# Moving gate projections into the first and last steps of a software-pipelined RWKV stage, one core of Trainium2

## The chip, the cores and the metric

One core of one Trainium2 chip runs the whole program in one launch. The time is the device time in microseconds (us). TensorE does the matmuls, VectorE (DVE), ScalarE (ACT) and GpSimd (POOL) the rest; weights come from device memory (DRAM) by DMA, issued from the SP queue, and small transfers are issued from ACT's queue.

## The reference, cut to what matters

Two transformer blocks, one after the other, on 512 tokens of width 1024, all in float32. The stage at issue is the first block's mixer:

```python
h = rmsnorm(x, norm_mix_pre)
f_att, f_rwkv, f_gate = split(h @ w_in)               # 2304, 3328 and 2048 columns
o_att  = dilated_window_attention(q, k, v, rel_bias)  # of f_att
o_rwkv = rwkv7_time_mix(token_shift(f_rwkv, mu), ...) # 16 heads of 64: r, k, v and three small low-rank inputs
gates  = sigmoid(f_gate + b_gate)                     # gate 0 and gate 1, 1024 columns each
merged = gates[0] * (o_att @ w_att_branch) + gates[1] * (o_rwkv @ w_rwkv_branch)
x = x + rmsnorm(merged @ w_out, norm_mix_post)
```

`token_shift` mixes each projected row with the row before it, per channel. Inside `rwkv7_time_mix` a 64x64 state per head runs over the tokens; the kernel does it in 4 chunks of 128 tokens, with a triangular inverse per chunk and head. A feed-forward part follows, and then the second block.

## The kernel before, in words

Every float32 projection is done as three float32r matmuls (lines 526 to 528: high times high, high times low, low times high). Weights come in 126 units of 128 x 2048 float32 (1 MB) through a ring of three buffers. For each unit ACT writes the rounded high part (`hi`, line 1123), and then POOL (line 517), or for ten of the units DVE (`weights_low`, line 1772), writes what is left, the low part.

The stage has these parts in order: q, k and v projections; the dilated attention; then steps -2 to 7 of the RWKV part (`step(p)`, one such function in each engine's program). The 16 RWKV heads are 8 pairs. Step p works on three pairs at once: pair c = p + 2 is prepared (low-rank inputs, decay, key norms), for pair b = p + 1 the triangular inverse is built over seven levels (`level_x`, `level_t`, line 862 and lines 870 and 872), and for pair a = p the four chunks are run through the state (`chunk_rhs`, `chunk_solve`, `chunk_out`) and normalised. So steps -2 and -1 lack a, step -2 lacks b as well, step 6 has no c and step 7 only a. The branch projections `attb` and `rwkvb` follow.

The remaining projections of `h` fill the gaps. They are cut into 42 halves of units: a half is 8 pieces, each three matmuls with 512 columns. They are two low-rank inputs, r, k and v of each pair (24), gate 0 (8) and gate 1 (8). Sixteen are done beside the attention. The other 26 are spread over the steps by `advance(early, n)` and `advance(late, n)`: two in steps -2, -1 and 5, four in each of steps 0 to 4, none in steps 6 and 7. In the steps all halves use bank 0, so the first piece of a half waits until the one before is taken out (`half_taken`). A half of r, k or v is taken by ACT (`stage`, line 1247, into the single buffer GT) and then by DVE (`shift`, lines 1729 and 1730); a gate half by ACT alone (a sigmoid into GT, line 1254 or 1263), which then stores it to DRAM. After every second half ACT runs `hi` for the unit two further on.

The order on each engine is written out by hand and engines wait for each other by semaphores. In step -2 ACT takes both last gate 0 halves before the exponentials of pair 0, and waits for a store before it takes the second, since both use GT. Units 21 and 22 (`attb` and the first of `rwkvb`) have their low parts made by POOL in step 5. Before step 6 ACT issues the loads of both gates from DRAM, into the buffers of the high and low parts of `h`, which no half needs any more.

Of the kernel before, what the change touches and what calls it, by code (L numbers as in the profile page):

```python
# [49 lines left out]
STAGES = [("qk", 6, 6), ("v", 3, 3), ("lora", 1, 0), ("rwkv_first", 4, 0), ("gate0", 4, 0), ("rwkv", 12, 0),  # L50
# [4 lines left out]
SIDE = ("lora", "rwkv_first", "gate0", "rwkv")  # L55

PACKED = ("qk", "v", "lora", "rwkv_first", "rwkv", "gate0", "attb", "rwkvb", "wout", "ffn", "pool", "q2", "kv2",
          "group", "gatep", "gatea", "poolb", "attnb", "wout2", "ffn2")
UNIT0, USE0, UNITS, USES = {}, {}, {}, {}
# [8 lines left out]
def packed_order():  # L68

    at, place = 0, {}  # L70
    for name in PACKED:
        count = UNITS[name]
# [14 lines left out]
    return [place[name, u] for name, count, _ in STAGES for u in range(count)]  # L87
# [80 lines left out]
def build(nc, x, wpack, lora_wa, lora_g, params, rel_bias, post_gains, sink, ctab, btab, icount, out):  # L168
# [7 lines left out]
    with ExitStack() as ctx:  # L176
# [202 lines left out]
        source = packed_order()  # L379


        DVE_LO0, DVE_LO1 = UNIT0["rwkv"] + 2, UNIT0["rwkv"] + UNITS["rwkv"]
# [10 lines left out]
        def half(pair, part):  # L393

            return 2 + 4 * pair + part + (2 * UNITS["gate0"] if pair >= 2 else 0)

        GATE0 = 10

        def half_taken(n):

            if n < 2:
                return shifted, n + 1
            if GATE0 <= n < GATE0 + 8:
                return gated, 2 + n - GATE0 + 1
            late = n >= GATE0 + 8
            pair, part = (n - 2 - 8 * late) // 4, (n - 2 - 8 * late) % 4
            return (gated, pair + 1 + 8 * late) if part == 3 else (shifted, 2 + 3 * pair + part + 1)
# [80 lines left out]
        def _(sp):  # L488
            def load(n):
                if n >= RING:  # L490
                    sp.wait_ge(*freed[n - RING])
                sp.dma_start(raw[:, n % RING, :], wpack[source[n]]).then_inc(unit_in[n % RING], 16)
# [28 lines left out]
        def _(pe):  # L521
# [227 lines left out]
            def later_halves(n0, n1):  # L749
                for n in range(n0, n1):  # L750
                    yield from side_half(n, 0, n - 1)
# [204 lines left out]
            def step(p):  # L956
# [3 lines left out]
                if p == -2:  # L960
                    early = later_halves(GATE0 + 6, GATE0 + 8)
                else:
                    early = later_halves(half(c, 2), half(c, 2) + (2 if 2 <= c < PAIRS else 0))
                late = later_halves(half(c + 1, 0), half(c + 1, 0) + (2 if 2 <= c + 1 < PAIRS else 0))
# [4 lines left out]
                if has_a:  # L969
                    chunk_rhs(a, 0)  # L970
                advance(early, 2)
# [4 lines left out]
                advance(early, 2)  # L976
                if has_a:
                    chunk_out(a, 0)
                for t in range(1, NT):
# [4 lines left out]
                    advance(early, 1)  # L984
                    if has_c:
                        if t == 1:
                            lora_z(c, 1)
                        elif t == 2:
                            key_sums(c)
                        else:  # L990
                            key_roots(c)
# [4 lines left out]
                    advance(early, 1)  # L996
                    if has_a:
                        chunk_out(a, t)
                    advance(early, 2)
# [4 lines left out]
                advance(late, 1)  # L1004
# [4 lines left out]
                advance(late, 3)  # L1009
# [3 lines left out]
                advance(late, 1)  # L1013
# [5 lines left out]
                advance(late, 3)  # L1019
# [3 lines left out]
                advance(late, 1)  # L1023
# [5 lines left out]
                advance(late, 2)  # L1029
                if has_c:  # L1030
                    gate_z(a, c)
                advance(late, 1)
# [3 lines left out]
                advance(late, 2)  # L1036
# [4 lines left out]
                advance(late, 2)  # L1041
                assert next(early, None) is None and next(late, None) is None
# [71 lines left out]
        def _(act):  # L1114
# [5 lines left out]
            def hi(n):  # L1120

                act.wait_ge(unit_in[n % RING], 16 * (n // RING + 1))
# [1092 lines left out]
```

## Time and profile before

| | us |
|---|---|
| three runs of the kernel | 2155.59, 2163.86, 2168.63 (median 2163.86) |
| the profiled execution | 2157.88 |
| its span | 2156.1 |
| TensorE busy | 2025.7 (94%) |
| VectorE busy | 890.8 (41%) |
| ScalarE busy | 792.5 (37%) |
| GpSimd busy | 537.1 (25%) |
| mean granted TensorE clock | 0.93 of full |

The page shows busy time per engine, the span in 40 slices with the busy share and the granted clock, the chain of work that ended last, and the costliest groups of instructions. TensorE's matmuls are pipelined, so its busy time holds latencies that overlap; the rate of work is read from the starts of neighbouring matmuls. "PE" is TensorE.

### The profile page before, as it was taken

The page shows a single profiled execution, that of the slowest core. Times are in us where ns is not written, and L with a number is a line of the kernel's source. Part 1 is how long each engine was busy: PE and PEld are TensorE (multiplying, and loading weights), DVE is VectorE, ACT ScalarE, POOL GpSimd, SP SyncE. Part 2 cuts the span into 40 slices and gives each one's busy share as a digit, 9 for nine tenths or more (in the row PEclk, how much of TensorE's full clock was granted, in tenths as well). Part 3 has the DMA queues.
Part 4 walks back from the last instruction along what each step waited for, and adds up shares of the span by engine and source line. Part 5 has one row for each costly group of instructions (what it writes and reads, how often), then busy time and mean ns, then how long its engine had stood idle before and what let it go on. Part 6 is the DMA issues. An engine that isn't in the chain of part 4 may idle for free.

```text
span 2156.1 us, 24479 instructions
## 1 busy us (share of the span) xinstructions
PE 2025.7 (94%) x10404; PEld 1651.9 (77%) x10404; DVE 890.8 (41%) x1439; ACT 792.5 (37%) x1142; POOL 537.1 (25%) x120
## 2 busy tenths in 40 slices
PE   7999977999999989989989999989899999999998
PEld 5877756778777777877878888878566778888886
DVE  2023335666666666543331144450566432012243
ACT  5235544354354344231342222242465333222222
POOL 2431210000000000002434444433222343444442
PEclk9999995999899998568999999999999999999999
DMA  4621120010010010201332222223111222222222
GB/s 154 221 74 56 67 79 11 23 47 25 23 47 25 23 45 25 79 1 69 117 108 98 98 98 96 94 84 107 39 59 59 84 83 99 97 97 98 98 98 78
DMA packets 31281, 160.80 MB, mean 75 GB/s; under 512 B 3103, under 2 KB 5535, under 8 KB 14916
## 3 DMA queue, kind: packets, MB, share of 16 engines
q1 hardware_dynamic: 19244, 135.40, 18.4%
q10 hardware_dynamic: 11928, 23.83, 3.2%
q8 instruction: 83, 1.36, 0.3%
q14 instruction: 26, 0.21, 0.0%
HBM read 152.63 MB, written 10.25 MB: 76 GB/s over the span
## 4 chain that ended last, share of the span: by engine, by line
PE 83%; DVE 10%; ACT 4%; issue 1%; DMA 1%; POOL 0%; DVEq 0%; ACTq 0%
PE ps L526 21%; PE ps L528 20%; PE ps L527 20%; PE ps L872 2%; PE ps L870 2%; PE ps L619 2%; PE ps L862 2%; PE ps L641 2%; DVE stat L1705 1%; DVE level L1845 1%; PE ps L633 1%; PE ps L912 1%; PE ps L902 1%; PE ps L793 1%; PE ps L950 1%
## 5 line engine op out<-in xcount | busy, mean ns | idle before, releaser
L517 POOL TENSOR_TENSOR w_lo<-w_raw,w_hi 128x2048 fp32r<-128x2048 f32 x116 | 536.9, 4629 | 1588.9 <-ACT w_hi L1123 1588.9
L526 PE MATMUL ps<-ht_hi,w_hi 128*128 128x512 f32 (+1 forms) x1304 | 529.3, 406 | 36.5 <-DVE rkv L1730 22.3
L528 PE MATMUL ps<-ht_hi,w_lo 128*128 128x512 f32 (+1 forms) x1304 | 504.4, 387 | 0.0
L527 PE MATMUL ps<-ht_lo,w_hi 128*128 128x512 f32 (+1 forms) x1304 | 504.3, 387 | 0.0
L1123 ACT ACTIVATE w_hi<-w_raw 128x2048 fp32r<-128x2048 f32 x126 | 241.0, 1914 | 493.6 <-PE ps L528 437.6
L526 PEld LDWEIGHTS ps<-ht_hi,w_hi 128*128 128x128 f32 x1304 | 251.9, 193 | 114.4 <-issue 53.3
L528 PEld LDWEIGHTS ps<-ht_hi,w_lo 128*128 128x128 f32 x1304 | 251.8, 193 | 49.6
L527 PEld LDWEIGHTS ps<-ht_lo,w_hi 128*128 128x128 f32 x1304 | 252.9, 194 | 40.2 <-issue 1.4
L2052 DVE TENSOR_TENSOR hid_lo<-hidden,hid_hi 128x1024 fp32r<-128x1024 f32 x27 | 129.3, 4789 | 149.1 <-ACT hid_hi L1485 149.1
L526 PE MATMUL ps<-w_hi,hid_hi 128*128 128x512 f32 x432 | 168.2, 389 | 0.0
L528 PE MATMUL ps<-w_hi,hid_lo 128*128 128x512 f32 x432 | 168.1, 389 | 0.0
L527 PE MATMUL ps<-w_lo,hid_hi 128*128 128x512 f32 x432 | 168.0, 389 | 0.0
L1346 ACT ACTIVATE tinv_t<-ps 128x512 fp32r<-128x512 f32 x96 | 57.7, 601 | 117.5 <-PE ps L872 117.5
L526 PEld LDWEIGHTS ps<-w_hi,hid_hi 128*128 128x128 f32 x432 | 81.1, 188 | 16.9
L527 PEld LDWEIGHTS ps<-w_lo,hid_hi 128*128 128x128 f32 x432 | 81.1, 188 | 16.8
L528 PEld LDWEIGHTS ps<-w_hi,hid_lo 128*128 128x128 f32 x432 | 81.1, 188 | 16.8
L526 PE MATMUL ps<-w_hi,ht_hi 128*128 128x512 f32 (+2 forms) x256 | 86.7, 339 | 2.1 <-POOL w_lo L517 2.1
L528 PE MATMUL ps<-w_hi,ht_lo 128*128 128x512 f32 (+2 forms) x256 | 86.5, 338 | 0.0
L527 PE MATMUL ps<-w_lo,ht_hi 128*128 128x512 f32 (+2 forms) x256 | 86.3, 337 | 0.0
L1867 DVE TENSOR_TENSOR xinv<-ps,consts 128x512 fp32r<-128x512 f32 x96 | 62.5, 684 | 45.0 <-PE ps L862 44.4
L1845 DVE TENSOR_TENSOR level<-gram_inv,consts 128x512 fp32r<-128x512 f32 x112 | 80.5, 760 | 0.6
L2061 DVE TENSOR_TENSOR hidden<-ps,gate_act 128x1024 f32<-128x1024 f32 x16 | 19.6, 1225 | 135.3 <-ACT gate_act L1524 135.3
(253 smaller groups left out, 2814.7 us busy)
## 6 DMA issues: line engine op xcount, KB each, us to landing
w_raw<-in_wpack SPq DMA_DIRECT2D x126, 1024.0 KB, 4.9
bias_skewed_dram<-bias_rows_dram ACTq DMA_DIRECT2D x1, 3840.0 KB, 22.4
toe<-bias_skewed_dram ACTq DMA_DIRECT2D x1, 3072.0 KB, 13.0
gate_dram<-gate_tile ACTq DMA_DIRECT2D x10, 256.0 KB, 5.0
x_res<-in_x SPq DMA_DIRECT2D x4, 512.0 KB, 6.5
merged<-gate_dram ACTq DMA_DIRECT2D x1, 2048.0 KB, 8.7
gate<-gate_dram ACTq DMA_DIRECT2D x1, 2048.0 KB, 14.7
x_res<-in_x ACTq DMA_DIRECT2D x1, 2048.0 KB, 8.8
```

The costliest lines, as they stand in the source:

```text
L517: nc.gpsimd.tensor_tensor(Wl[:, slot, :], raw[:, slot, :], f32(Wh[:, slot, :]), ALU.subtract).then_inc(lo_ready, 1)
L526: mm(dst, wh, ah, start=first, stop=False)
L527: mm(dst, wh, al, start=False, stop=False)
L528: return mm(dst, wl, ah, start=False, stop=last)
L619: last = mm(bank(s["bank"], s["n"]), s["q"], s["k"], start=True, stop=True)
L641: last = mm(out_slot(a, i), v, PT[:, j, :], start=j == 0, stop=j == len(it["vals"]) - 1)
L862: last = mm(ps[:, 4 + h, tok(t)], Mb[h][:, t, :], Tb[h][:, t, :] if lv else identR[:], start=True, stop=True)
L1123: actf(Wh[:, n % RING, :], raw[:, n % RING, :], ACT.Copy).then_inc(hi_ready, 1)
L1346: actf(TT[h][:].rearrange("p a b -> p (a b)"), bank(6 + h), ACT.Copy)
L1845: inc(v.tensor_tensor(Mb[h][:], GA[h][:], lmask(lv), ALU.mult), "m_ready")
L1867: inc(v.tensor_tensor(Xb[h][:], b3(4 + h), cast4(ident), ALU.add), "x1_ready")
L2052: v.tensor_tensor(HIl[:, 2 * g:2 * g + 2, :], HID[:, 2 * g:2 * g + 2, :], f32(HIh[:, g % RING, :, :]), ALU.subtract).then_inc(hid_lo, 1)
```

## The change

The halves get an explicit order (`HALVES`) and each step a list of halves (`STEP_HALVES`). Beside the attention: the low-rank inputs, r, k, v of pairs 0 and 1, and all of gate 0. Step -2: gate 1 halves 0 and 1. Step -1: two halves of pair 2. Steps 0 to 4: three halves each, all r, k or v. Step 5: v of pair 7 and gate 1 half 2. Step 6: three gate 1 halves. Step 7: the last two. How many pieces run at each of 21 places in a step is in three tables. TensorE's `chunk_rhs(a, 0)` now comes ahead of `inverse_grams(b)`, and the first pieces of a step after `level_x(b, 0)` and after `chunk_out(a, 0)`; `key_roots` moves behind `level_t(b, 3)`. The last half of a step is taken at the start of the next. Gate 1 halves 2 to 7 each get a buffer of their own. Twelve units are loaded as two strided halves of 512-byte rows. DVE makes the low parts of 13 units (10 to 22) and none is left to POOL inside the steps. The loads of the two gates move into step 7, behind the last stored gate half.

```diff
+HALVES = ([("lora", 0, 0), ("lora", 0, 1)] + [("rkv", pair, part) for pair in range(2) for part in range(3)]
+          + [("gate0", u, 0) for u in range(8)] + [("gate1", u, 0) for u in range(2)]
+          + [("rkv", pair, part) for pair in range(2, PAIRS) for part in range(3)]
+          + [("gate1", u, 0) for u in range(2, 8)])
...
+STEP_HALVES = {-2: (16, None, 17), -1: (18, None, 19), 5: (35, None, 36), 6: (37, 38, 39), 7: (40, 41, None)}
+STEP_HALVES.update({p: (20 + 3 * p, 21 + 3 * p, 22 + 3 * p) for p in range(5)})
+
+SLOTS3 = (0, 1, 2, 1, 1, 1, 1, 1, 0, 1, 1, 2, 1, 2, 1, 1, 1, 2, 1, 1, 2)
+SLOTS2 = (0, 1, 2, 1, 1, 1, 1, 1, 0, 0, 0, 0, 1, 1, 1, 1, 1, 1, 1, 1, 0)
+SLOTS_LAST = (2, 2, 2, 1, 1, 0, 1, 2, 1, 2, 2, 0, 0, 0, 0, 0, 0, 0, 0, 0, 0)
...
-        DVE_LO0, DVE_LO1 = UNIT0["rwkv"] + 2, UNIT0["rwkv"] + UNITS["rwkv"]
+        DVE_LO0, DVE_LO1 = UNIT0["rwkv"] + 1, UNIT0["rwkvb"] + 1
...
+                if split_load(n):
+                    halves = raw[:, n % RING, :].rearrange("p (k j c) -> p j k c", k=KT, j=2)
+                    for j in range(2):
+                        u, h = half_place(places, side_halves(n)[j])
+                        sp.dma_start(halves[:, j], wpack[u].rearrange("p (k j c) -> p j k c", k=KT, j=2)[:, h]
+                                     ).then_inc(unit_in[n % RING], 16)
...
             def step(p):                                   # TensorE
...
+                if has_a:
+                    chunk_rhs(a, 0)
                 if has_b:
                     inverse_grams(b)
                 if has_c:
                     lora_z(c, 0)
-                if has_a:
-                    chunk_rhs(a, 0)
-                advance(early, 2)
+                fill()
                 if has_a:
                     chunk_solve(a, 0)
                 if has_b:
                     level_x(b, 0)
-                advance(early, 2)
+                fill()
                 if has_a:
                     chunk_out(a, 0)
+                fill()
...
                     if has_b:
                         level_t(b, t)
-                    advance(early, 1)
+                    if has_c and t == 3:
+                        key_roots(c)
+                    fill()
                     if has_a:
                         chunk_out(a, t)
-                    advance(early, 2)
+                    fill()
...
+            def take_gate1(u):                             # ScalarE
+
+                n = HALF["gate1", u, 0]
+                buf = GT[:] if u < 2 else (SZ, CS, KK, E, T1, X2)[u - 2][:]
                 act.wait_ge(side_full, n + 1)
-                if pair:
-                    act.wait_ge(gate_stored, 16 * pair)
+                if u == 1:
+                    act.wait_ge(gate_stored, 16)
+                elif u == 2:
+                    act.wait_ge(rs["kb_ready"], PAIRS)
...
+            def take_half(n):
...
+                if kind == "rkv":
...
+                    stage(n, 0, GT[:], 8 * part + pair)
                 else:
+                    take_gate1(pair)
+                if n % 2:
+                    hi(unit_behind(n))
...
             def step(p):                                   # ScalarE
...
+                if p > -2:
+                    take_half(STEP_HALVES[p - 1][2])
                 if has_a:
                     rhs(a, 0)
...
                 if has_a:
                     rhs(a, 1)
+                if p == 7:
+                    take_half(STEP_HALVES[p][0])
...
                 if has_c:
                     key_root(c)
+                if p < 7:
+                    take_half(STEP_HALVES[p][0])
                 if has_a:
                     rhs(a, 3)
...
                 if has_b:
                     tokens(b, 2)
+                take_half(STEP_HALVES[p][1])
+                if p == 7:
+                    act.wait_ge(gate0_stored[0], 16 * 4)
+                    act.wait_ge(gate0_stored[1], 16 * 4)
+                    act.dma_start(MG[:], gate0_dram.rearrange("k p t -> p k t")).then_inc(gate_back[0], 16)
+                    act.wait_ge(gate_stored, 16 * PAIRS)
+                    act.dma_start(G1[:], gate1_dram.rearrange("k p t -> p k t")).then_inc(gate_back[1], 16)
+                if has_b:
                     level(b, 5)
-                if late:
-                    shift_part(c + 1, 0)
                 if has_a:
                     deviation(a)
                     widen_norm(a)
...
             def step(p):                                   # VectorE
...
                 if has_a:
                     state(a, 2)
+                shift_half(first)
                 if has_c:
-                    bonus_terms(c)
-                    decay_args(c)
                     key_root(c)
                 if has_b:
                     level_x(b, 3)
                 if has_a:
                     solved(a, 3)
                 if has_c:
-                    key_norm(c)
+                    bonus_terms(c)
+                    decay_args(c)
                 if has_b:
                     level_mask(b, 4)
                 if has_c:
+                    key_norm(c)
                     rates(c)
+                weights_behind(first)
...
+                shift_half(middle)
                 if has_b:
                     grams(b, 0)
...
+                weights_behind(middle, 0)
                 if has_a:
                     normed(a)
                 if has_b:
                     grams(b, 2)
+                weights_behind(middle, 1)
```

## Rows read from the trace of the kernel before

**Rows 1.** The page: clock granted to TensorE in 40 slices, in tenths of full.
```profile
PEclk9999995999899998568999999999999999999999
```

**Rows 2.** Windows: busy time by engine, clock, DMA; steps -2, -1, 0, 2, 5, 6, 7.
```profile
297.80:334.40 36.60, 21.26 (x70) 13.15 (x70) 13.19 (x21) 11.86 (x16) 6.04 (x2) 0.73 0.16 53
334.40:398.10 63.70, 58.36 (x306) 49.66 (x306) 38.15 (x74) 23.83 (x41) 0.00 (x0) 0.71 0.01 3
398.10:476.50 78.40, 74.30 (x486) 60.98 (x486) 50.16 (x97) 35.14 (x56) 0.00 (x0) 0.93 0.10 33
...
554.90:637.10 82.20, 78.60 (x488) 63.42 (x488) 50.21 (x97) 35.20 (x56) 0.00 (x0) 0.88 0.10 31
...
793.90:875.60 81.70, 69.48 (x438) 57.82 (x438) 53.55 (x93) 34.37 (x54) 9.45 (x2) 0.81 0.10 32
875.60:945.90 70.30, 67.89 (x371) 59.55 (x371) 34.71 (x69) 22.62 (x37) 0.00 (x0) 0.59 0.16 58
945.90:978.60 32.70, 25.64 (x134) 18.96 (x135) 8.91 (x15) 2.60 (x7) 0.00 (x0) 0.54 0.00 1
```

**Rows 3.** Timeline of TensorE, two pieces: start us, duration us, line, operands.
```profile
496.68 0.39 PE L526 MATMUL ps<-ht_hi,w_hi 128*128 128x512 f32 x1
496.91 0.40 PE L527 MATMUL ps<-ht_lo,w_hi 128*128 128x512 f32 x1
...
560.74 0.63 PE L528 MATMUL ps<-ht_hi,w_lo 128*128 128x512 f32 x1
561.16 0.63 PE L526 MATMUL ps<-ht_hi,w_hi 128*128 128x512 f32 x1
```

**Rows 4.** Waits of TensorE, 298 to 979 us: total us, times, longest us.
```profile
PE ps L526 <- DVE rkv L1730: 22.3, 16, 5.3
PE ps L821 <- ACT rwkv_gate L1341: 9.9, 1, 9.9
PE ps L862 <- DVE level L1845: 9.6, 10, 4.7
```

**Rows 5.** Timeline of ScalarE in step -2; in brackets idle time before, and releaser.
```profile
319.84 1.28 ACT L1263 ACT_TABLE_LOAD   x1 [2.85 <-PE ps L528]
321.13 0.69 ACT L1263 ACTIVATE gate_tile<-ps,params_sb 128x512 f32<-128x512 f32 x1
...
325.42 1.91 ACT L1123 ACTIVATE w_hi<-w_raw 128x2048 fp32r<-128x2048 f32 x1 [3.60 <-DMA gate_dram<-gate_tile]
327.35 1.28 ACT L1331 ACT_TABLE_LOAD   x1
```

**Rows 6.** Timeline of VectorE: the pair of level masks in step 2, twice in 5.
```profile
557.52 1.29 DVE L1845 TENSOR_TENSOR level<-gram_inv,consts 128x512 fp32r<-128x512 f32 x2
...
796.50 5.40 DVE L1845 TENSOR_TENSOR level<-gram_inv,consts 128x512 fp32r<-128x512 f32 x2
...
846.02 5.60 DVE L1845 TENSOR_TENSOR level<-gram_inv,consts 128x512 fp32r<-128x512 f32 x2
```

**Rows 7.** Timeline of GpSimd in step 5.
```profile
796.25 4.50 POOL L517 TENSOR_TENSOR w_lo<-w_raw,w_hi 128x2048 fp32r<-128x2048 f32 x1 [464.34 <-ACT w_hi L1123]
845.52 4.95 POOL L517 TENSOR_TENSOR w_lo<-w_raw,w_hi 128x2048 fp32r<-128x2048 f32 x1 [44.77 <-ACT w_hi L1123]
```

**Rows 8.** Instructions on the tile of raw weights: ns min/median/max, first and last start.
```profile
L1772 DVE TENSOR_TENSOR w_lo<-w_raw,w_hi x10: 2281/2285/2286, 409.4 to 772.2; 128x2048 fp32r<-128x2048 f32 x10
```

**Rows 9.** Timeline of ScalarE at the end of step 7.
```profile
970.51 0.60 ACT L1355 ACTIVATE rwkv_out<-ps 128x512 f32<-128x512 f32 x1 [2.92 <-PE ps L925]
976.65 0.27 ACT L1359 ACTIVATE root<-ps,consts 128x8 f32<-128x8 f32 x1 [5.54 <-PE ps L793]
```

**Rows 10.** DMA issues: KB each, median us from issue to landing.
```profile
w_raw<-in_wpack SPq DMA_DIRECT2D x126, 1024.0 KB, 4.9
...
toe<-bias_skewed_dram ACTq DMA_DIRECT2D x1, 3072.0 KB, 13.0
gate_dram<-gate_tile ACTq DMA_DIRECT2D x10, 256.0 KB, 5.0
```

**Rows 11.** Timeline of VectorE at the start of step 7.
```profile
946.83 3.88 DVE L2015 TENSOR_TENSOR rwkv_lo<-rwkv_out,rwkv_hi 128x3584 fp32r<-128x3584 f32 x1
```

More of the change, by code:

```diff
@@ L86, in packed_order, with half_place @@
                 at += 1
-    return [place[name, u] for name, count, _ in STAGES for u in range(count)]
+    return place
+def half_place(place, what):
+    kind, i, part = what
+    if kind == "lora":
+        return place["lora", 0], part
+    if kind == "gate0":
+        return place["gate0", i // 2], i % 2
+    if kind == "gate1":
+        return place["pairs", 2 * i + 1], 1
+    return place["pairs", 2 * i + part // 2], part % 2
 PCOLS = [("mu", 26), ("w0", 8), ("a0", 8), ("k_k", 8), ("k_a", 8), ("r_k", 8), ("ln_w", 8), ("ln_b", 8),
@@ L959, in step, with fill @@
                 has_a, has_b, has_c = 0 <= a, 0 <= b < PAIRS, c < PAIRS
[L960 to L964, printed above, removed]
+                halves = step_halves(p)
+                slots = iter(SLOTS_LAST if p == 7 else SLOTS2 if None in STEP_HALVES[p] else SLOTS3)
+                def fill():
+                    advance(halves, next(slots))
+                if has_a:
+                    chunk_rhs(a, 0)
                 if has_b:
@@ L1003, in step @@
                     to_tokens(b, 1)
-                advance(late, 1)
+                fill()
                 if has_a:
@@ L1008, in step @@
                     level_t(b, 4)
-                advance(late, 3)
+                fill()
                 if has_b:
@@ L1018, in step @@
                     grams(b, 0)
-                advance(late, 3)
+                fill()
                 if has_b:
@@ L1022, in step @@
                     grams(b, 1)
-                advance(late, 1)
+                fill()
                 if has_a:
@@ L1035, in step @@
                     grams(b, 3)
-                advance(late, 2)
+                fill()
                 if has_c:
@@ L1040, in step @@
                     refine_c(b)
-                advance(late, 2)
-                assert next(early, None) is None and next(late, None) is None
+                fill()
+                assert next(halves, None) is None and next(slots, None) is None
             for p in range(-2, PAIRS):
```

167 lines of the change are left out of this document (78 added, 89 removed).

## The prediction

> **What bounds the kernel now.** I read the slices of the page first. TensorE is busy almost everywhere, but its clock is not: of 40 slices the seventh has 5 tenths, and the 16th to 19th have 8, 5, 6, 8 [rows 1]. These are the two ends of the RWKV steps, so I cut that stretch into one window per step [rows 2]. The reader is to see three things. Steps 0, 1, 3 and 4 take 78.4 us each, with TensorE busy for 74.3 and a clock of 0.93 (step 2: 82.2 us, 0.88). Step 5 has half as many projection halves (two, not four) and yet takes 81.7 us. The end steps run at low clock: 0.73 and 0.71 in steps -2 and -1, 0.59 and 0.54 in steps 6 and 7. The clock has two levels, 1.2 and 2.4 GHz, so a mean of 0.71 over 63.7 us means (1 - 0.71) x 2 x 63.7 = 37 us at the lower one. By the same sum the ten steps hold 20 + 37 + 4 x 11 + 20 + 31 + 58 + 30 = 240 us at the lower level in 680.8 us.
>
> Then the timeline, for what a half costs. Neighbouring matmuls of 512 columns start 0.23 us apart at the upper level and 0.42 to 0.43 at the lower [rows 3]. A half has 24 of them: 5.6 us at the upper, 10.2 at the lower.
>
> Then the waits of TensorE over the ten steps [rows 4]: 22.3 us for VectorE's token shift (16 times), 9.9 once for ScalarE's gate copy, 9.6 for level masks, and the timelines of the engine waited for [rows 5 to 7]. So TensorE's work in a fixed order sets the time in steps 0 to 4, and at the ends it is latency, a stalled VectorE and the low clock.
>
> **The change part by part.** The sum goes against the profiled execution, 2157.88 us (span 2156.1), which is 6 us under the median of the three runs, 2163.86.
>
> *Steps 0 to 4: one half fewer each.* This removes 5.6 us of TensorE's work per step. It also takes the first pieces behind the first chunk's output, so that the wait at a step's start for the shift (22.3 us in 16 waits, 1.4 each) goes. What is late next is VectorE: `inverse_grams` is now behind `chunk_rhs`, its two predicated copies and the pair of masks (1.29 [rows 6]) must end before `level_x(b, 0)`, and no piece stands between. I put 1.5 to 2 us there, so the two cancel. The remaining pieces are thinner (12 in the first half of the step, where there were 16) and can't all cover what 16 did: some waits grow, and the low-clock stretch of 11 us may. Bounds per step: -7.5 (the half, the wait and a little clock) to +1 (all of it lost again in waits and low clock; step 5, with two halves and 81.7 us, shows that a step can be that poor). I take -4.5, nearest to the plain removal since TensorE is 95% busy: -22.5 for five.
>
> *Step -2: the second gate half is taken a step later.* Before, ScalarE loads the sigmoid table (1.28), takes the half (0.69), waits for the store of it (3.60) and runs `hi` (1.91) before the exponentials [rows 5]; the gate copy is behind these, and TensorE waits 9.9 us for that [rows 4]. This 7.5 us leaves the chain. What is late next: the first gate half, with a table load, is now ahead of the widening of the key norms, on which `key_roots` waits; and the second half's pieces come behind that. Bounds -11 to -2; I take -6.
>
> *Step -1.* Two halves as before, but one moves to the front, where TensorE had none, and ran 37 us at the lower level. Less its waits that is some 31 us of work that could take 15.5: bounds -16 (all at the upper level) to 0 (none). Each inverse level has a chain through VectorE and ScalarE that a faster clock doesn't shorten, and 8 pieces in a row are followed by a stretch with none. I take the middle, -8.
>
> *Step 5: POOL leaves.* Two pairs of level masks take 5.40 and 5.60 us where the same pair takes 1.29 [rows 6], and at exactly these times GpSimd makes a low part, 4.50 and 4.95 us [rows 7]: 8.4 us of VectorE stall, and behind each the low clock (31 us at the lower level in this step). VectorE now makes these parts, at 2.29 us each [rows 8]; three units more, 6.9 us in all, on an engine that is 64% busy in steps 0 to 4 and does fewer there. A clean step with two halves should be a clean step less two: 78.4 - 11.2 = 67.2. I take 68.7, so -13; bounds -7 (one stall's worth kept) to -16.
>
> *Step 6: three halves into a step at half clock.* 58 of its 70.3 us are at the lower level. Own work at the upper: 12 + (58 - 2 of waits) / 2 = 40; with three halves 40 + 17 = 57, the lower end (-13). If the clock stays where it is, 3 x 10.2 = +31, the upper end. That steps 0 to 4 hold 0.93 with the same kind of mixture speaks for the first; they also lose 4 us to waits and 5 to the clock, of which I count 8, and ScalarE takes a gate (table 1.28, 0.69) ahead of the first right-hand side. 57 + 8 = 65: I take -5.
>
> *Step 7: two halves, and what comes behind them.* Its first 25 us are four chunks, each a chain of TensorE, ScalarE, TensorE, VectorE. At the lower level they fill the time; at the upper the 16 pieces (11.3 us) fit in what is freed. VectorE is held by `rwkv_lo` (3.88 [rows 11]) at the start either way. So 0 for the chunks. But after the last chunk ScalarE must now load the sigmoid table, take the last half (0.69), run `hi` (1.91), wait for the store (5.0 from issue to landing [rows 10]) and issue two loads before the deviation, and load the square root's table again. With the copy: 0.60 + 1.28 + 0.69 + 5.0 + about 1 for the issues + 1.28 = 9.9 us, where it had 6.1 from 970.51 to 976.65 [rows 9]. Nothing covers it, since `norm_roots` stands ahead of `attb` in TensorE's order: +4. VectorE's last low part (2.29) also stands ahead of the products of `attb`: up to +2, I take +1. Bounds for the step -3 to +16 (chunks at the lower level with pieces of 10.2 us per half). I take +5.
>
> On table switches row and page differ. In the trace the load takes 1.28 us and the next instruction starts at once, 319.84 + 1.28 = 321.12 against 321.13 [rows 5]. The Trainium skill ("ScalarE: Activation LUTs", What ACT_TABLE_LOAD costs) adds a drain of 1380 ns for every switch, 2.66 us in all; by that the tail of step 7 would be 2.8 us longer, and the sum +3. I go by the row.
>
> *Loads in two strided halves: 0.* Twelve units now come as 512-byte rows. No row shows such a load. A whole unit lands in 4.9 us, the table of biases, 3 MB in rows of 2 KB, in 13.0 [rows 10], 4.3 per MB; four times as many rows can at worst make it 17. Two halves pass between the freeing of a buffer and its `hi`, some 19 us beside the attention and over 40 in the steps. I take 4.9 to 6, hidden; the upper end costs nothing either unless the attention's waits line up, up to +5.
>
> *Attention.* Sixteen halves before, sixteen now, eight of them gates both times: 0, within 3 either way.
>
> Sum: -22.5 - 6 - 8 - 13 - 5 + 5 = -49.5, which is 2108.4 against 2157.88, and 2114.4 against the median. A check from the other side: lost in the ten steps now are half of 240 us of low clock, 120, and the 42 us of the three waits; steps 0 to 4 hold some 9 us each of that, so the five end steps hold about 115. If these become like steps 0 to 4, with 9 to 12 each, 55 to 70 come back, less the 5 of the new tail and less what the thinner steps lose. I say **2110 us**.
>
> **The rivals.**
>
> *The thinner steps give nothing.* The order of a step is fixed, and its chain of seven levels may be what takes 78 us; then the removed half only turns into waits. For it: 4 us of waits per step already, all for VectorE, and step 5. Against: those waits are for the shift, which pieces cause themselves, and the masks of step 5 were stalled by GpSimd. Time: 2110 + 22.5 = 2132.
>
> *The moved halves are not hidden.* Steps 6 and 7 keep their clock: +31 and +16 instead of -5 and +5, 47 us more: 2157. For it: 58 of 70 us in step 6 at the lower level. Against: in step 6 nothing dense was there to hold the clock, and now 24 dense pieces are.
>
> *Slower: the clock falls in the steps that were thinned.* Place: steps 0 to 4, where 32 dense pieces become 24. Price: each us that passes to the lower level costs half a us of work; if each of these steps went to the share of step -1 (0.71, 45 us low instead of 11) it would lose 17 and gain 5.6, 11 net, 57 for five. With steps -2, -1 and 5 gaining only 20 and the ends of steps 6 and 7 at +10 this is 2157.9 + 57 - 20 + 10 = 2205. It decides from 22 us low per step: then a thinned step gains nothing.
>
> *It does not do what it says.* The pieces stand behind other waits in step 5 and step -2, and these keep their length: then only steps 0 to 4 and the POOL part count, 2157.9 - 22.5 - 8 + 5 = 2132, the same number as the first rival by another way.
>
> **How the numbers follow.** Forecast as described 0.62 (own range 2085 to 2128); first and fourth rival together 0.20 (2128 to 2145); moved halves not hidden 0.11 (2145 to 2165); slower 0.07. A change under 0.5% (10.8 us) can't be told from none. Faster: 0.62 + 0.20 + 0.04 of the third = 0.86; same 0.07; slower 0.07. The range takes in the forecast's bounds and the first rival: 2082 to 2146.
>
> **What would show it right or wrong.** Windows by step: 73 to 75 us in steps 0 to 4, under 70 in step 5 with no GpSimd work in it, clock above 0.8 in steps -1, 5 and 6. The pair of masks never above 1.4 us. TensorE's 9.9 us wait in step -2 down to a few. Between the last chunk and `attb` about 4 us more than now, with ScalarE as the releaser. It is wrong if steps 0 to 4 stay at 78, or if step 6 is over 80.

## The result: 2063 us, and the profile after

| | before | after |
|---|---|---|
| median (lowest to highest), runs | 2163.62 us (2155.59 to 2168.63), 4 | 2063.26 us (2061.77 to 2066.38), 4 |
| the profiled execution, its span | 2157.88, 2156.1 | 2061.77, 2060.0 |

The ratio is 0.9541, with a 95% interval of 0.951 to 0.9573: 100 us less. The ratios leave out runs over 1.5% above the fastest of their kernel, so they can differ a little from the quotient of two medians. The forecast had half of that (2110), and the time lies below its range.

The page of the kernel after: busy time by engine, then the clock in 40 slices.

```profile
PE 1962.3 (95%) x10404; PEld 1592.9 (77%) x10404; DVE 887.4 (43%) x1446; ACT 786.0 (38%) x1139; POOL 523.1 (25%) x117
...
PEclk8999998999999989999999999999999999999999
...
w_raw<-in_wpack SPq DMA_DIRECT2D x114, 1024.0 KB, 4.9
w_raw<-in_wpack SPq DMA_DIRECT2D x24, 512.0 KB, 5.3
```

The 5 in the seventh slice is an 8, and of the run of 8, 5, 6, 8 near the end of the steps one 8 is left [rows 1]. A half of a unit lands in 5.3 us, a whole one in 4.9.

The windows of the kernel after, steps -2 to 5 one by one, then steps 6 and 7 together up to the first matmul of `attb`. Columns as in [rows 2]: start:end, length, busy time by engine, clock, share of DMA, GB/s. From step -1 on a window begins at the first matmul of `inverse_grams`. In the kernel after, a step's `chunk_rhs(a, 0)` stands ahead of that, so its 1.8 us lie in the window of the step before.

```profile
297.80:328.90 31.10, 23.10 (x68) 15.40 (x68) 12.88 (x23) 9.99 (x15) 3.24 (x1) 0.73 0.08 24
328.90:385.80 56.90, 50.08 (x316) 42.70 (x316) 40.63 (x75) 27.82 (x45) 0.00 (x0) 0.91 0.15 45
385.80:453.50 67.70, 66.28 (x466) 53.47 (x464) 50.27 (x97) 31.22 (x53) 0.00 (x0) 0.97 0.07 19
...
520.70:587.30 66.60, 65.18 (x464) 52.48 (x462) 50.30 (x97) 32.17 (x54) 0.00 (x0) 1.00 0.10 32
...
721.10:789.40 68.30, 65.21 (x441) 53.27 (x440) 47.48 (x93) 30.41 (x51) 0.00 (x0) 0.90 0.06 16
789.40:883.70 94.30, 86.51 (x614) 69.79 (x613) 47.79 (x85) 37.29 (x56) 0.00 (x0) 0.96 0.20 68
```

| step | -2 | -1 | 0 | 1 | 2 | 3 | 4 | 5 | 6 and 7 | sum |
|---|---|---|---|---|---|---|---|---|---|---|
| before, us | 36.6 | 63.7 | 78.4 | 78.4 | 82.2 | 78.4 | 78.4 | 81.7 | 103.0 | 680.8 |
| after, us | 31.1 | 56.9 | 67.7 | 67.2 | 66.6 | 67.3 | 66.5 | 68.3 | 94.3 | 585.9 |
| before, at the lower level | 20 | 37 | 10 | 10 | 20 | 10 | 10 | 31 | 88 | 237 |
| after, at the lower level | 17 | 10 | 3 | 3 | 0 | 3 | 0 | 14 | 8 | 59 |

The last two lines are worked out from the clock as in the prediction, (1 - clock) x 2 x length, with the clock unrounded (the two digits of the windows gave the prediction's 240). Over the whole stretch the same 26 halves run, so that no projection work has gone. It takes 94.9 us less, with 178 us less at the lower level. If all of these had been full of matmuls, they would be worth half, 89 us; some were waits, which a faster clock doesn't shorten, so 89 is an upper end. By the windows TensorE's busy time fell by 64.7 us (618.4 to 553.7) and its idle time by 30.2 (62.4 to 32.2).

The waits of TensorE in the same stretch of the kernel after (total, times, longest):

```profile
PE ps L834 <- DMA lora_w<-in_lora_g: 7.6, 1, 7.6
PE ps L845 <- ACT norm_sq L1366: 6.4, 2, 3.9
PE ps L908 <- DVE level L1904: 6.2, 8, 1.3
PE ps L916 <- DVE xinv L1926: 3.9, 2, 3.3
...
PE ps L571 <- DVE rkv L1780: 2.3, 8, 0.4
```

The wait for the shift fell from 22.3 to 2.3 us, the gate copy's 9.9 is not among them any more, and the masks' longest is 1.3 instead of 4.7 [rows 4].

### The profile page after: what moved, and what is told of

Read it like the earlier page. It is cut to its first block, busy times and chain, and to the rows that moved or that the text cites. A ratio compares the mean times of both kernels' runs of the same rounds, so it can differ in the third digit from the quotient of the medians.

```text
span 2060.0 us, 24487 instructions
## 1 busy us (share of the span) xinstructions
PE 1962.3 (95%) x10404; PEld 1592.9 (77%) x10404; DVE 887.4 (43%) x1446; ACT 786.0 (38%) x1139; POOL 523.1 (25%) x117
## 4 chain that ended last, share of the span: by engine, by line
PE 84%; DVE 8%; ACT 5%; issue 2%; DMA 1%; POOL 0%; SPq 0%; ACTq 0%; DVEq 0%
PE ps L571 22%; PE ps L572 21%; PE ps L573 21%; PE ps L664 2%; PE ps L686 2%; PE ps L908 2%; PE ps L918 2%; PE ps L916 2%; DVE stat L1755 1%; PE ps L678 1%; DMA w_raw<-in_wpack 1%; PE ps L948 1%; PE ps L945 1%; PE ps L996 1%; PE ps L925 1%
## 5 line engine op out<-in xcount | busy, mean ns | idle before, releaser
L562 POOL TENSOR_TENSOR w_lo<-w_raw,w_hi 128x2048 fp32r<-128x2048 f32 x113 | 522.9, 4629 | 1506.7 <-ACT w_hi L1171 1506.6
L1904 DVE TENSOR_TENSOR level<-gram_inv,consts 128x512 fp32r<-128x512 f32 x112 | 72.0, 684 | 0.6
L1235 ACT ACTIVATE probs_t<-ps 128x384 f32<-128x384 f32 (+2 forms) x64 | 29.7, 483 | 102.6 <-PE ps L678 102.4
```

What stands on the lines that cost most here:

```text
L562: nc.gpsimd.tensor_tensor(Wl[:, slot, :], raw[:, slot, :], f32(Wh[:, slot, :]), ALU.subtract).then_inc(lo_ready, 1)
L1904: inc(v.tensor_tensor(Mb[h][:], GA[h][:], lmask(lv), ALU.mult), "m_ready")
```

## The experiments

Each kernel starts from the one before (`b_`) or the one after (`a_`). Its ratio is to runs of the kernel before on the same chip, with a 95% interval. "us low" is time at the lower clock level, from the windows.

### POOL's part alone: b_masks_free

```diff
-        DVE_LO0, DVE_LO1 = UNIT0["rwkv"] + 2, UNIT0["rwkv"] + UNITS["rwkv"]
+        DVE_LO0, DVE_LO1 = UNIT0["rwkv"] + 2, UNIT0["rwkvb"] + 1
```

> The kernel before, with the low parts of units 21 and 22 made by VectorE instead of GpSimd (leaves nothing out). Theory (step 5 loses its time to the two stalled pairs of masks and to the low clock behind them): step 5 goes from 81.7 to 68 to 70 us, 2163.6 - 13 = 2151. Rival (only the stall itself goes, the low clock stays): 8 us, 2156. If VectorE's added 4.6 us count instead: 2160 or more.

Measured: 2171.24 us (2159.53 to 2184.6, 10 runs), ratio 0.9965 [0.9923, 1.0007]. The mask pair in step 5, from VectorE's timeline:

```profile
859.88 1.29 DVE L1845 TENSOR_TENSOR level<-gram_inv,consts 128x512 fp32r<-128x512 f32 x2
```

Its windows of step 1 and step 5:

```profile
479.30:564.70 85.40, 81.65 (x488) 66.94 (x488) 50.35 (x97) 35.33 (x56) 0.00 (x0) 0.84 0.09 30
...
810.60:885.70 75.10, 69.77 (x438) 58.06 (x438) 49.74 (x95) 34.38 (x54) 0.00 (x0) 0.84 0.11 34
```

All pairs of masks in step 5, of which two took 5.40 and 5.60 us [rows 6], take 1.28 or 1.29, so GpSimd was the cause. The Trainium skill ("SBUF — State Buffer", "SBUF: two separate sides") has the two engines share a pair of ports that one of them holds for a whole instruction; the trace agrees: the two stalled pairs end at 801.90 and 851.62 us, each 1.15 us after GpSimd's instruction (800.75 and 850.47) [rows 6, 7]. Step 5 fell from 81.7 to 75.1 us, half of the 13 that the stalls and the clock behind them seemed to hold, and nearest to the rival. Over whole runs the interval includes no change at all. The first window belongs to the finding below: step 1, which the edit doesn't touch, took 85.4 us here and 78.4 in the profile of before.

### The removed half alone: b_three_halves

```diff
+            SHORT = [half(pair, 3) for pair in range(2, 7)]
...
+                    if n in SHORT and k < KT - 1:
+                        yield
+                        continue
```

> The kernel before, with five gate 1 halves (one in each of steps 0 to 4) cut to one piece of eight; leaves out seven eighths of these five projections. Theory P (the placement of the pieces in a step keeps the clock up, not their number): steps 0 to 4 still have about 10 us at the lower level, 78.4 - 4.9 = 73.5 us each, 2163.6 - 25 = 2139. Theory N (with one half fewer the step is short and clean by itself): 67 to 68 us each, 2163.6 - 55 = 2109. Theory D (thinner steps lose their clock, as the prediction feared): 76 us or more each, 2155.

Measured: 2194.31 us (2191.59 to 2202.95, 10 runs), ratio 1.0099 [1.006, 1.0139]. With some 25 us less work it is slower. One of its steps:

```profile
572.10:658.00 85.90, 81.59 (x467) 67.29 (x467) 50.31 (x97) 35.55 (x56) 0.00 (x0) 0.78 0.09 30
```

Steps 0 to 4 take about 85 us each, with 38 us low. So the prediction's slower rival is a real mechanism: with the pieces at their old places, fewer of them lose the clock. But the cut is harsher than the change's own thinning. The seven pieces that go all stand at chunks 2 and 3, which are left with one piece between them, while the kernel after takes four pieces from each half of the step and spreads the rest. The profiled execution is also the slowest of the ten, 9 us over their median. TensorE counts as busy for 95% of this window.

### The order alone: b_pieces_behind

```diff
-                advance(early, 2)
...
+                advance(early, 2)
```

Of the four first pieces of a step, the two ahead of `level_x(b, 0)` go behind it, and the two behind it follow `chunk_out(a, 0)`.

> The kernel before, with one edit in TensorE's order: the first two pieces of a step run behind level_x(b, 0) instead of ahead of chunk_solve(a, 0), and the next two behind chunk_out(a, 0); 32 pieces in a step as before, leaves nothing out. Theory P1 (this placement is what keeps the clock in steps 0 to 4): 72 to 74 us a step with 3 to 7 us at the lower level, some -25 to -30 against before. Theory P2 (placement over the whole step matters, the late pieces and key_roots too): the stretch at 10 us low stays, 77 to 79 us a step, no change beyond 5.

Measured: 2143.97 us (2142.17 to 2144.33, 4 runs), ratio 0.9887 [0.9849, 0.9926]. One step:

```profile
550.90:626.00 75.10, 72.45 (x488) 59.43 (x488) 50.20 (x97) 35.15 (x56) 0.00 (x0) 0.95 0.11 34
```

Moving four pieces by one place, with nothing removed, takes steps 0 to 4 from 395.8 to 378.9 us (75.2, 75.1, 75.1, 78.3, 75.2), 16.9 less. By whole runs it is more, 25.6 us between the medians, since the profiled execution of before was one of its faster ones.

### Both on the kernel before: b_three_behind

The edits of the last two together.

> The kernel before with both edits: the five gate halves cut to one piece (seven eighths of these projections left out), and the first four pieces of a step moved behind level_x(b, 0) and chunk_out(a, 0). With the halves cut alone a step took 85 us, 38 of them at the lower level. Theory P (a stretch without dense pieces puts the clock down, wherever it is): with nine pieces left for the first half of a step chunks 2 and 3 are still bare, so 79 to 84 us a step with over 20 low; 2175 or more. Theory P1 (only the first four pieces' places matter): 70 to 72 us a step, 2130.

Measured: 2150.8 us (2147.12 to 2151.72, 4 runs), ratio 0.9887 [0.9812, 0.9962].

```profile
556.40:634.30 77.90, 75.00 (x465) 62.63 (x465) 50.20 (x97) 35.33 (x56) 0.00 (x0) 0.85 0.10 33
```

Steps of 74.9 to 79.6 us, with 17 to 27 us low: with the half gone, these places are still not as good as those of the kernel after. Both theories missed, at 2175 and 2130. The ratio is that of b_pieces_behind: at these places 25 us less work bought nothing. Steps 0 to 4 take 390.1 us here and 335.3 in the kernel after, with about as many pieces. The difference, 55 us, lies in what else the change does there: the even spread of the remaining pieces, r, k and v halves only, and the new order on VectorE and ScalarE. No run separates these.

### The kernel after, with four halves in steps 0 to 4: a_four_halves

```diff
-                for k in range(KT):
+                again = 4 if 20 <= n < 35 and (n - 20) % 3 != 1 else 0
+                for j in range(again + KT):
```

Eight pieces more per step are repeated; their result isn't used. A table of its own gives the places, none of them ahead of `level_x(b, 0)`.

> The changed kernel, with eight pieces more in each of steps 0 to 4 (the first four pieces of the first and of the last half are run twice, the first time for nothing), so 32 pieces a step as in the kernel before. Theory P (placement): 67.2 + 5.6 = 72.8 us a step at a clock of 0.97 or more, 2063.3 + 28 = 2091. Theory N (number): the low-clock stretch and the waits of before come back, 77 to 78 us a step, 2063.3 + 53 = 2116.

Measured: 2097.51 us (2095.34 to 2100.01, 4 runs), ratio 0.9607 [0.9544, 0.967]. Two steps:

```profile
535.10:609.50 74.40, 73.09 (x490) 59.68 (x488) 50.28 (x97) 32.34 (x54) 0.00 (x0) 0.95 0.09 29
609.50:681.90 72.40, 71.28 (x490) 57.87 (x488) 48.55 (x95) 31.78 (x52) 0.00 (x0) 0.98 0.07 18
```

Steps 0 to 4 take 371.0 us with as many pieces as before, where they took 395.8: 24.8 us come from everything in the change but the count. From there to 335.3 it is 35.7 us, 7.1 per step, for the half. That is more than its 5.6 of work, since 37 us low become 10.

### The kernel after, with pieces at the front again: a_pieces_front

```diff
+SLOTS_EARLY = (2, 2, 0, 1, 1, 1, 1, 0, 0, 1, 1, 2, 1, 2, 1, 1, 1, 2, 1, 1, 2)
```

used in steps 0 to 4 in place of `SLOTS3`, which begins 0, 1, 2 and has 1 at the eighth place.

> The changed kernel, with four of the pieces of the first half in steps 0 to 4 moved to where they stood before: two ahead of chunk_solve(a, 0), two behind level_x(b, 0), none behind chunk_out(a, 0), and the stretch of chunks 1 and 2 with one fewer. Theory P1: each step gets a stretch of 10 us or more at the lower level and a wait for the shift at its start back, 67 to 73 us, 2063.3 + 30 = 2093. Theory P2: 1 to 2 us a step for the wait alone, 2070.

Measured: 2101.61 us (2100.03 to 2104.66, 4 runs), ratio 0.9695 [0.9657, 0.9734]; 38 us over the kernel after.

```profile
537.90:613.70 75.80, 72.09 (x465) 58.78 (x462) 50.49 (x97) 32.30 (x54) 0.00 (x0) 0.89 0.09 29
613.70:684.60 70.90, 67.36 (x464) 54.85 (x462) 48.33 (x95) 31.77 (x53) 0.00 (x0) 0.95 0.07 18
```

Moving pieces without changing their count costs 8 us per step and leaves 7 to 24 us low in each. Of the parts undone one at a time this one cost the most, a little ahead of the removed halves (2097.51 us with them back).

### The chunk's and the roots' order undone: a_order_undone

`chunk_rhs(a, 0)` goes back behind the low-rank matmuls, `key_roots` back ahead of `chunk_solve(a, 3)`.

```diff
-                if has_a:
-                    chunk_rhs(a, 0)
...
+                        else:
+                            key_roots(c)
```

> The changed kernel, with TensorE's chunk_rhs(a, 0) put back behind lora_z and key_roots put back ahead of chunk_solve(a, 3), pieces as changed. Theory P1: the order of the small parts is worth little, since the clock comes from the pieces: 0 to +2 us a step, 2063 to 2073. Theory P2 (the clean clock needs this order, because key_roots waits for the root of the key norms in a stretch without pieces): +4 to +6 us a step, 2085 or more.

Measured: 2064.69 us (2063.05 to 2065.01, 4 runs), ratio 0.9522 [0.9477, 0.9566]: the same as the kernel after. Two steps:

```profile
586.50:654.40 67.90, 67.13 (x464) 55.00 (x464) 48.25 (x96) 31.39 (x53) 0.00 (x0) 0.95 0.06 18
654.40:719.70 65.30, 64.44 (x464) 52.22 (x464) 50.27 (x98) 32.92 (x54) 0.00 (x0) 1.00 0.12 33
```

Most of its steps take 65.3 to 65.4 us, with nothing low, and so are better than after's 66.6; steps 0 and 3 fall for 10 and 7 us. The early `chunk_rhs` costs something: at the start of after's steps TensorE waits 0.72 us for the masks, where no piece stands between.

```profile
389.14 1.26 PE L908 MATMUL ps<-ident_r,level 128*128 128x128 f32 x8 [0.72 <-DVE level L1904]
...
390.62 0.47 PE L571 MATMUL ps<-ht_hi,w_hi 128*128 128x512 f32 x1 [0.21 <-DVE rkv L1780]
```

### The moved halves taken out: a_no_moved

```diff
+                    if n >= 37 and k < KT - 1:
+                        yield
+                        continue
```

> The changed kernel, with the five halves of steps 6 and 7 cut to one piece of eight; leaves out seven eighths of these five projections. 35 pieces are 24.6 us at the upper level. Theory (the pieces hold the clock, so the chains beside them run at 2.4 GHz): steps 6 and 7 stay at 90 to 103 us together at a mean clock of 0.6 (94.7 with the halves), 2063.3 + 0 to + 8. Rival (the pieces only fill the time, the clock is kept by something else): 94.7 - 24.6 = 70 us, 2039.

Measured: 2068.12 us (2066.39 to 2069.49, 4 runs), ratio 0.9475 [0.9423, 0.9527]. Steps 6 and 7 together:

```profile
788.50:887.30 98.80, 87.65 (x509) 71.85 (x508) 47.92 (x85) 37.81 (x56) 0.00 (x0) 0.66 0.19 61
```

With 24.6 us less work these steps are 4.5 us longer than after's: 67 us low instead of 8.

### Work added to the kernel before: b_idle_pieces

In steps 6 and 7 of the kernel before, 24 and 16 pieces more, at the places that the kernel after uses:

```diff
+                    for _ in range(next(slots)):
+                        mm3(bank(0), Wh[:, 0, 0:P], Wl[:, 0, 0:P], Wh[:, 1, 0:T], Wl[:, 1, 0:T], True, True)
```

> The kernel before with work added that nobody reads: 24 pieces of three 512-column matmuls in step 6 and 16 in step 7, at the places of the changed kernel, between weights that lie in the buffers anyway, into bank 0. 40 pieces are 28.1 us at the upper level. Nothing else is changed. Theory (steps 6 and 7 are slow for want of a clock, and pieces bring it): steps 6 and 7 go from 103 to 94 to 97 us, low clock from 88 to about 10 us, so the kernel with more work is faster: -6 to -9 us. Rival (the added work costs what it takes): +20 to +28.

TensorE also gets a wait in step 6 for the low parts that the added matmuls read.

Measured: 2164.02 us (2160.03 to 2182.04, 10 runs), ratio 0.9947 [0.9909, 0.9986]. Steps 6 and 7 together, first of the kernel before, then with the pieces:

```profile
875.60:978.60 103.00, 93.52 (x504) 78.51 (x505) 43.62 (x83) 25.23 (x44) 0.00 (x0) 0.57 0.11 40
```

```profile
888.70:982.90 94.20, 90.58 (x625) 73.54 (x625) 42.89 (x83) 24.60 (x44) 0.00 (x0) 0.94 0.12 43
```

28.1 us of matmuls (40 pieces of 0.70) that nobody reads make the stretch 8.8 us shorter. That is about the kernel after's 94.3. In the profiles of the other `b_` kernels, with the code of before in these two steps, they took 98 to 108 us, so the gain is 4 us at the least. At these places the work is paid for by the clock, and whether it is useful makes no difference.

### The store wait alone: b_no_store_wait

```diff
-                    act.wait_ge(gate0_stored[0], 16 * 4)
-                    take_gate0(7, 0, GT[:])
-                    act.wait_ge(gate0_stored[1], 16 * 4)
+                    take_gate0(7, 0, BON[1][:])
```

The last half goes to a buffer that is free there; the waits stand at the start of step -1.

> The kernel before, with the last gate 0 half of step -2 taken into a buffer of its own, so that ScalarE doesn't wait for the store of the half (the two waits for stores move to the start of step -1). Leaves nothing out. Theory: 3.6 us less in step -2 (36.6 to 33) and nothing elsewhere, since step -1 keeps its pieces late and its 37 us of low clock: -4. Rival (step -2's wait is what puts step -1 at the lower level): -4 and a further -8 to -15 in step -1.

Measured: 2172.62 us (2158.6 to 2176.55, 10 runs), ratio 0.9997 [0.9965, 1.003].

```profile
PE ps L821 <- ACT rwkv_gate L1341: 5.4, 1, 5.4
```

```profile
297.80:331.20 33.40, 21.50 (x70) 13.32 (x70) 14.09 (x23) 11.99 (x16) 7.22 (x2) 0.76 0.19 59
331.20:397.20 66.00, 60.66 (x306) 51.73 (x306) 38.08 (x74) 24.08 (x41) 0.00 (x0) 0.68 0.01 3
```

The window of step -2 shrinks by 3.2 us; counted from its first matmul, which here starts 1.1 us later (301.33 against 300.28), it is 4.2. Step -1 loses 2.3, with 42 us low instead of 37: a wait removed gave almost nothing while the clock behind it stayed low.

### A version that spreads the rest: a_spread_tail

```diff
+SLOTS_SPREAD = (0, 1, 2, 1, 1, 1, 1, 1, 0, 1, 0, 1, 1, 0, 1, 0, 1, 1, 1, 1, 0)
```

in steps -1 and 5, without `SLOTS2`'s four empty places in a row. In step 7 `hi` and the wait for the last store move behind the normalisation, and so does the last low part on VectorE.

> The changed kernel with two repairs, leaves nothing out. In steps -1 and 5 the second half's eight pieces begin at chunk 3 instead of behind level_x(b, 4), so that no stretch of a step is without pieces: low clock of 10 and 14 us down to 3 each, 4 to 9 us less in all. In step 7 ScalarE's weight split and the wait for the last stored gate go behind the deviation and its widening, and VectorE's low part behind the normalisation: 1 to 2 us less. 2063.3 - 7 = 2056. Rival (these stretches are short of VectorE and ScalarE, not of pieces): 2062 or more.

Measured: 2060.91 us (2058.72 to 2061.55, 4 runs), ratio 0.9504 [0.9467, 0.9542]. Step 5:

```profile
719.80:783.80 64.00, 60.41 (x440) 48.25 (x438) 47.32 (x93) 30.12 (x51) 0.00 (x0) 1.00 0.06 17
```

The time lies between the theory's 2056 and the rival's 2062. Step 5 goes from 68.3 to 64.0 us, none of it low. Step -1 (57.5) and steps 6 and 7 (93.7) hardly move.

### The best version: a_best

a_spread_tail, and `chunk_rhs(a, 0)` back behind the low-rank matmuls; `key_roots` stays late.

> The changed kernel with the two repairs of a_spread_tail, and chunk_rhs(a, 0) put back behind lora_z, where it covers the wait of level_x(b, 0) for the level masks; key_roots stays late. Undoing both gave steps of 65.3 us where the clock held and 68 to 70 where it didn't. Theory (key_roots' place keeps the clock, chunk_rhs' place costs the wait): 65.5 us in all of steps 0 to 4, 2060.9 - 8 = 2053. Rival (it is chunk_rhs' place that keeps the clock at a step's start): some steps fall to the lower level, 2060 to 2066.

Measured: 2051.47 us (2049.05 to 2053.37, 4 runs), ratio 0.9436 [0.9351, 0.9522]. Steps -2 to 3:

```profile
298.00:326.90 28.90, 22.97 (x70) 15.51 (x72) 11.25 (x21) 9.83 (x14) 1.14 (x1) 0.73 0.09 26
326.90:383.20 56.30, 48.97 (x306) 41.19 (x308) 40.05 (x75) 26.66 (x44) 0.00 (x0) 0.91 0.12 37
383.20:448.30 65.10, 64.22 (x464) 52.33 (x465) 50.29 (x98) 31.56 (x53) 0.00 (x0) 1.00 0.09 25
...
515.90:581.00 65.10, 64.21 (x463) 52.33 (x463) 50.29 (x98) 32.97 (x54) 0.00 (x0) 1.00 0.12 35
581.00:645.70 64.70, 64.07 (x462) 52.28 (x462) 48.16 (x96) 31.03 (x53) 0.00 (x0) 1.00 0.07 19
```

Against a_spread_tail, `chunk_rhs` alone has moved, and the median is 9.4 us lower; the places of the pieces are the same. The four runs of a_best all lie below the four of the kernel after, by 8 us or more, though the two were not run together and their intervals to the kernel before overlap. Four of the five middle steps have nothing low, the other (step 1) 7 us; over the ten steps it is 45 us. Its steps 0 to 4 take 327.8 us, after's 335.3.

## Why the prediction was wrong

| term | forecast | measured |
|---|---|---|
| steps 0 to 4 | -22.5 | -60.5 |
| step -2 | -6 | -5.5 |
| step -1 | -8 | -6.8 |
| step 5 | -13 | -13.4 |
| steps 6 and 7 | -5 + 5 = 0 | -8.7 |
| loads, attention, rest | 0 | about -1.2 |

The last line is what is left of 2157.88 - 2061.77 = 96.1 us. Of the 46.6 us between forecast and measurement 38.0 stand in the first line.

*Steps 0 to 4: the step that failed.* The prediction put "-7.5 (the half, the wait and a little clock) to +1" per step and took -4.5; it was -12.1. The half was sized rightly (5.6 us at the upper level). The error was to read the re-placed first pieces as a wait only, "so the two cancel", and to let the clock change for the worse alone ("the low-clock stretch of 11 us may" grow). Neither held. The waits for the shift did not cost 1.4 us per step. In steps 0 to 4 of the kernel before (398.1 to 793.9 us) they are:

```profile
PE ps L526 <- DVE rkv L1730: 16.5, 14, 1.7
```

That is 3.3 us per step, of which 0.5 are left, and the new wait for the masks costs 0.7 instead of 1.5 to 2. TensorE's idle time in these five steps fell from 20.0 to 6.5 us. And the clock rose: the lower level fell from 61 to 10 us. The 60.5 us are 28.1 of the halves' work, 13.5 of idle time and 18.9 by which the rest of the busy time shrank (the fall of the low time could give 25.6 at most).

In steps, by kernel: 395.8 us before, 378.9 with four pieces per step moved (b_pieces_behind), 371.0 with all of the change but the count (a_four_halves), 335.3 with the eight pieces gone too. Undoing the places alone costs 38 us (a_pieces_front). So the lower bound of the term left out the 11 us of low clock that every step had, and even with them (another -5.5 per step) it holds -12.1 only just, at -13.

Thinning with the pieces at their old places was a loss (b_three_halves, 1.0099 [1.006, 1.0139]), as the slower rival said, though that run leaves a barer stretch than the change would. The rival's place was right; its price was about 27 us low more per step than the profile of before had in four of the five. It also said that 22 us low would eat the gain of a half, and 38 gave a slower kernel. It didn't come about because the same change moved the pieces. The rival treated the places as fixed, and so did the first one, by which the removed half would turn into waits.

*Step -2.* The size was near, the mechanism right in part. The gate copy's wait of 9.9 us is gone, and the late next wait is the one that the prediction named, for the widening of the key norms. In the kernel after (297 to 329 us):

```profile
PE ps L845 <- ACT norm_sq L1366: 2.5, 1, 2.5
```

Before it was 0.4. The longest wait of the step, for the DMA of the low-rank weights, is 7.6 us and was 7.8 before. In the profile of after the attention ends 1.7 us later (its last group of matmuls starts at 291.83 against 290.12), within what executions of the kernels with before's code show (290.1 to 293.4). Counted from its first matmul (300.28 and 301.87) the step shrank by 7.1 us.

*Step -1.* The middle between 0 and -16 was near: 37 us low became 10. The window is 6.8 us shorter and holds 1.8 us of step 0's `chunk_rhs`, so that 8.6 came back, of the 13.4 that the clock could give at most. That the inverse's chain holds the rest was argued, not tried.

*Step 5.* The sum was right for a cause that was half right. GpSimd's leaving alone gives 6.6 us (b_masks_free), less than the 8.4 us of stall. The other 6.8 come with the rest of the change, which no run takes apart in this step. The clean step that I took as 67.2 is 64.0 if its pieces are spread (a_spread_tail).

*Steps 6 and 7.* "Three halves into a step at half clock" was forecast by its lower end at -13 and taken at -5, with +5 for step 7. Together they gained 8.7: 88 us low became 8, worth up to 40, against 28.1 us of work moved in. That the gain is not 12 is not for longer waits, since TensorE's idle time fell from 9.5 to 7.8 us; not all of the low time was work that the clock shortens. Step 6's `chunk_rhs` stands in the window before, so 6.9 of the 8.7 are the steps' own. a_no_moved and b_idle_pieces show from both sides that the moved halves cost less than nothing. The sum over the tail of step 7 was too high. ScalarE there, from the last chunk's output to the root, and TensorE's wait for it:

```profile
874.75 0.60 ACT L1405 ACTIVATE rwkv_out<-ps 128x512 f32<-128x512 f32 x1 [4.13 <-PE ps L971]
875.25 0.68 ACT L1306 ACTIVATE work_x<-ps,params_sb 128x512 f32<-128x512 f32 x1
876.33 1.91 ACT L1171 ACTIVATE w_hi<-w_raw 128x2048 fp32r<-128x2048 f32 x1 [0.40 <-ACT work_x L1306]
...
880.46 1.28 ACT L1409 ACT_TABLE_LOAD   x1 [2.22 <-DMA gate_dram<-work_x]
881.76 0.27 ACT L1409 ACTIVATE root<-ps,consts 128x8 f32<-128x8 f32 x1
```

```profile
882.98 1.11 PE L845 MATMUL ps<-consts,norm_sq 128*128 128x128 f32 x4 [3.88 <-ACT norm_sq L1366]
```

I had charged two table loads, 5.0 us for the store and 1 for the issues, 9.9 us from the copy to the root. It is 881.76 - 874.75 = 7.0: the sigmoid's table was still loaded, and of the store only 2.2 us stand behind `hi`. Before it was 6.1 [rows 9]. On the dearer table switch of the Trainium skill ("ScalarE: Activation LUTs", What ACT_TABLE_LOAD costs), which the prediction weighed, the rows decide against it: 880.46 + 1.28 = 881.74, and the root starts at 881.76. Nothing stands ahead of the load either: in [rows 5] `hi` ends at 327.33 and the load behind it starts at 327.35.

*Step by step against what I said would show it.* Step 5 under 70, masks never above 1.4, clock above 0.8 in steps -1, 5 and 6, and the 9.9 us wait gone: all so. Steps 0 to 4 at 73 to 75: they are at 67. About 4 us more between the last chunk and `attb`: it is 0.9 (8.1 us before, 970.51 to 978.63, and 9.0 after, 874.75 to 883.74), with ScalarE as the releaser.

## What to carry to other kernels

In this kernel the forecast failed on the clock, so, as far as one kernel can tell: where a stage shows any time at the lower TensorE clock, put into the bounds of every edit there, to the better as well, half of that time. Four pieces moved by one place gained 17 us in five steps, and seven removed at the wrong place lost time. Before thinning a stage, try the places first, by moving dense matmuls from where TensorE is well fed to behind the short dependent ones. And test a stage of low clock with unread dense matmuls: if it gets shorter, as here, work can be moved there at less than no cost.

## What the hardware showed that I had not expected

*Less work, more time, and the other way.* 25 us of matmuls fewer made a kernel slower by 1% (b_three_halves), and 28.1 us more made 8.8 us of difference to the better in their stretch (b_idle_pieces).

*The busy share does not tell the clock.* A window that was 95% busy ran at 0.78 (81.59 of 85.90 us, b_three_halves); one that was 94% busy ran at 1.00 (60.41 of 64.00, a_spread_tail). Nor does it take a long wait. The fall in step 1 of the kernel before comes behind a wait of 0.53 us. The second and third of the 512-column matmuls start 0.38 us apart and the next instruction follows 0.42 later, instead of 0.23 [rows 3]:

```profile
500.72 0.50 PE L526 MATMUL ps<-ht_hi,w_hi 128*128 128x512 f32 x1 [0.53 <-DVE rkv L1730]
501.06 0.58 PE L527 MATMUL ps<-ht_lo,w_hi 128*128 128x512 f32 x1
501.44 0.63 PE L528 MATMUL ps<-ht_hi,w_lo 128*128 128x512 f32 x1
501.86 1.70 PE L793 MATMUL ps<-consts,work_x 128*128 128x2 f32 x8
```

Ahead of this stand six 512-column matmuls (495.88 to 497.37) and then some 3 us of small ones, with no wait between them. Why the clock falls with one arrangement and holds with another that looks as busy, no run here settles; that it is the arrangement, the runs with equal work show.

*One program, several times.* A step with the code of the kernel before takes mostly 78.4, 82.2 or 85.3 us, with 10, 20 or 27 us low, and which of them differs between steps of the same code, and between executions (step 1: 78.4 in the one profile, 85.4 in b_masks_free, whose edit lies in step 5). Steps 0 to 4 took 395.8 us in the profile of before and 402.8, 409.7 and 415.5 in those of b_idle_pieces, b_masks_free and b_no_store_wait, whose edits lie elsewhere. So a gain read against the one profile of before is a low reading. Nineteen runs of the kernel before on one chip spread from 2158.09 to 2192.97 us, while the four of the kernel after lie within 5 us. Time at the lower level alone does not make a kernel unsteady: b_three_behind has 287 us of it in the ten steps, and its four runs lie within 5 us too.

*Left open.* Whether in the kernel after GpSimd could keep its three low parts, and how much the new order of pieces and the order of the first chunk would each bring without the other's table, wasn't tried. Nor is it known what in the rest of the change, besides the first four pieces' places, holds the clock in steps 0 to 4.
